# Expert loop of a fused two-block kernel: odd experts' input weights in four places of their own, TensorE looping over pairs of experts

## The reference, cut to what matters

```python
logits = hf @ w_router + b_router            # 32 experts, 4 chosen for a token
gates = softmax(top_k(logits, 4))
for each expert e, over the tokens that chose it:
    hc = xi @ w1[e] + b1[e]                  # 1024 -> 2048: gate and up
    g, u = hc[:, :1024], hc[:, 1024:]
    g = minimum(g, 7); u = clip(u, -7, 7)
    hm = (u + 1) * (g * sigmoid(1.702 * g))
    y += gate * (hm @ w2[e] + b2[e])         # 1024 -> 1024
x = x + g2 * y;  out = rms_norm(x, final_g)
```

## Time and profile before

| what | value |
|---|---|
| device time, median of 3 runs | 2288.06 us (2286.08 to 2289.45) |
| profiled execution: span from first to last instruction | 2379.3 us |
| profiled execution less the median of the runs shown | 91.2 us |
| busy, share of that span | PE 87%, DVE 41%, ACT 23%, POOL 21% |
| read from HBM | 782.55 MB, of which the 192 expert units 402.7 MB |
| passes in the expert loop | 33 (one expert of the 32 has two) |
| first matmul of the expert loop, last of it | 1409.9 us and 2372.0 us |

### The profile page before, as it was taken

The page is one execution under the profiler, slowest core; times in us unless marked ns, Lnnn a source line. Parts: engine busy times, 40 slices in busy tenths (PEclk is TensorE's granted clock), DMA queues, the critical chain, the costliest instruction groups (busy, mean ns, idle before and its releaser), DMA issues.

```text
span 2379.3 us, 27257 instructions
## 1 busy us (share of the span) xinstructions
PE 2070.6 (87%) x9038; PEld 1171.1 (49%) x9039; DVE 979.9 (41%) x2276; ACT 555.0 (23%) x1027; POOL 497.6 (21%) x562
## 2 busy tenths in 40 slices
PE   8998998967658576584999989999999999999998
PEld 7867887623223232232678854444444444444443
DVE  5955555646647566473375232111111111111112
ACT  4636301212112111122214222211111111121112
POOL 0000003466666666665300000000000000000000
PEclk9999999988878787896999989999999999999999
DMA  7352586799999999998842428799999999999996
GB/s 301 142 212 80 195 356 262 277 368 344 370 380 344 366 364 353 371 345 327 345 180 107 176 97 372 301 429 429 428 428 428 430 428 428 429 429 428 428 429 280
DMA packets 111703, 784.34 MB, mean 330 GB/s; under 512 B 13056, under 2 KB 13312, under 8 KB 80160
## 3 DMA queue, kind: packets, MB, share of 16 engines
q1 hardware_dynamic: 37920, 515.18, 52.3%
q0 software_dynamic: 73728, 268.47, 29.8%
HBM read 782.55 MB, written 1.05 MB: 329 GB/s over the span
## 4 chain that ended last, share of the span: by engine, by line
PE 75%; issue 11%; DVE 5%; another core or an unknown queue 2%; ACT 2%; POOL 2%; DMA 1%; DVEq 0%; ACTq 0%; POOLq 0%; SPq 0%
PE ps L786 56%; PE ps L945 16%; PE ps L1210 1%; DVE ring L1942 1%; DVE arena L1942 1%; DMA arena<-in_peer_v,arena 1%; PE ps L918 1%; POOL ring L746 1%; POOL ring L744 1%; DMA ring<-in_peer_v,arena 1%; DVE arena L1700 0%; DVE arena L1891 0%; ACT arena L1372 0%; PE ps L1241 0%
## 5 line engine op out<-in xcount | busy, mean ns | idle before, releaser
L786 PE MATMUL ps<-ring,arena 128*64 128x512 f32 (+2 forms) x3336 | 749.5, 589 | 41.8 <-issue 41.7
L786 PEld LDWEIGHTS ps<-ring,arena 128*64 128x64 f32 (+1 forms) x3336 | 262.9, 140 | 501.5 <-issue 500.7
L945 PE MATMUL ps<-ring,arena 128*128 128x512 f32 x768 | 366.5, 635 | 156.8 <-issue 134.7
L786 PE MATMUL ps<-arena,ring 128*128 128x256 f32 (+1 forms) x2272 | 486.2, 373 | 3.8 <-DVE arena L1685 3.2
L786 PEld LDWEIGHTS ps<-arena,ring 128*128 128x128 f32 x2272 | 417.4, 189 | 65.5 <-issue 6.9
L945 PEld LDWEIGHTS ps<-ring,arena 128*128 128x128 f32 x768 | 154.9, 204 | 364.6 <-issue 340.0
L945 PE MATMUL ps<-arena 128*128 128x512 f32 (+2 forms) x600 | 211.3, 599 | 66.5 <-ACT arena L1278 50.6
L1942 DVE CUSTOM_DVE_ANT_0 ring<-ring,ps 128x1024 f32<-128x1024 f32 x192 | 228.1, 1218 | 94.8 <-DMA ring<-in_peer_v,arena 88.5
L1600 ACT COPY arena<-ps 128x512 f32<-128x512 f32 (+1 forms) x165 | 89.2, 541 | 739.6 <-PE ps L786 683.5
L2255 DVE TENSOR_TENSOR arena<-ps,arena 128x512 f32<-128x512 f32 x66 | 45.7, 692 | 438.4 <-PE ps L1210 438.4
L786 PE MATMUL ps<-arena 128*128 128x128 f32 (+4 forms) x1502 | 215.2, 298 | 11.1 <-ACT arena L1262 6.6
(11 more groups left out here) (336 smaller groups left out, 1214.5 us busy)
## 6 DMA issues: line engine op xcount, KB each, us to landing
ring<-in_w_exp SPq DMA_DIRECT2D x192, 2048.0 KB, 17.1
ring<-in_w_in SPq DMA_DIRECT2D x24, 2048.0 KB, 9.5
ring<-in_w_ada SPq DMA_DIRECT2D x12, 2048.0 KB, 8.8
ring<-in_w_out SPq DMA_DIRECT2D x4, 2048.0 KB, 8.2
ring<-in_w_peer_q SPq DMA_DIRECT2D x4, 2048.0 KB, 10.6
ring<-in_w_br_rnn SPq DMA_DIRECT2D x4, 1280.0 KB, 7.4
ring<-in_w_br_attn SPq DMA_DIRECT2D x2, 2048.0 KB, 13.9
ring<-in_peer_u,arena POOLq DMA_INDIRECT x192
```

Of the source, the lines that this page charges most:

```text
L786: return pe.matmul(o, l, r, start=start, stop=stop)
L945: return pe.matmul(o, l, r, start=start, stop=False, skip_group_check=True)
```

## The change

Input weights (units 0 to 3) of odd experts get four more places, numbered 6 to 9: three at the end of the arena's reused part and one over `xT` and `hT`, which are dead by then. Even experts keep ring places 0 to 3. The output weights (units 4 and 5) of all experts still share places 4 and 5. SP now loads the inputs of expert 1 before the loop too, and in its loop, over pairs, those of e + 2 after the `Zg` and `Zu` of e, and the output weights of e + 1 after the `D` of e. PE loops over 16 pairs of experts; within a pair the pass's code stands twice (even and odd), each in an inner loop over that expert's passes, whose bounds PE reads from a new table `passes_to` that DVE writes. The region `M` is carved anew to make room; `final_row` moves to ring place 2 and is loaded after all weights.

```diff
-        arena_words = 27400
+        arena_words = 28608
+        x_start = at["fixed"]
         xT = carve("fixed", KD, T)
         hT = carve("fixed", KD, T)
...
+        more_slots = [arena[:, second + n * SLOT:second + (n + 1) * SLOT] for n in range(3)]
+        more_slots.append(arena[:, x_start:x_start + SLOT])
+        expert_slot = [ring[:, n * SLOT:(n + 1) * SLOT] for n in range(6)] + [more_slots[n] for n in (1, 2, 0, 3)]
+        w1_unit = [[expert_slot[n].rearrange("p (c j) -> p c j", c=KD) for n in places]
+                   for places in ((0, 1, 2, 3), (6, 7, 8, 9))]
+        w2_unit = [expert_slot[n].rearrange("p (c j) -> p c j", j=D) for n in (4, 5)]
+        final_row = expert_slot[2][:, 0:D]
...
-        w_full = [sem(f"expert_unit_loaded_{n}") for n in range(6)]
+        w_full = [sem(f"expert_unit_loaded_{n}") for n in range(10)]
...
-            def load(e, n):
-                sp.dma_start(ring[:, n * SLOT:(n + 1) * SLOT],
-                             a["w_exp"][bass.ds(e, 1), n].rearrange("e p w -> (e p) w")).then_inc(w_full[n], 16)
+            def load(e, n, place):
+                sp.dma_start(expert_slot[place],
+                             a["w_exp"][bass.ds(e, 1), n].rearrange("e p w -> (e p) w")).then_inc(w_full[place], 16)
...
             for n in sorted(range(RING), key=lambda slot: max(m for m in range(n_second) if m % RING == slot)):
+                if n == (n_second - 4) % RING:
+                    B.filled(sp, "o", HB - 1)
+                    load(1, 0, 6)
+                if n == (n_second - 3) % RING:
+                    load(1, 1, 7)
                 if n == (n_second - 2) % RING:
                     sp.wait_ge(s_mrg, 4 + 4)
-                    load(0, 5)
+                    load(0, 5, 5)
                 unit_free(sp, last_in_slot(n, n_second))
-                load(0, n)
+                load(0, n, n)
+            load(1, 2, 8)
+            B.filled(sp, "h3r", 3)
+            load(1, 3, 9)
             sp.wait_ge(s_slots, 1)
+
+            def used(e, job):
+                q = sp.value_load(last_of[0:1, bass.ds(e, 1)].bitcast(I32), min_val=0, max_val=MAX_PASSES - 1)
+                X.filled(sp, q, job)
+
+            with sp.Fori(0, E // 2 - 1) as p:
+                for odd, places in ((0, (0, 1, 2, 3)), (1, (6, 7, 8, 9))):
+                    e = p * 2 + odd
+                    used(e, "Zg")
+                    load(e + 2, 0, places[0])
+                    load(e + 2, 1, places[1])
+                    used(e, "Zu")
+                    load(e + 2, 2, places[2])
+                    load(e + 2, 3, places[3])
+                    used(e, "D")
+                    load(e + 1, 4, 4)
+                    load(e + 1, 5, 5)
+            used(E - 2, "D")
+            load(E - 1, 4, 4)
+            load(E - 1, 5, 5)
             sp.dma_start(final_row, a["final_g"].partition_broadcast(P)).then_inc(s_row, 16)
-            with sp.Fori(1, E) as e:
-
-                q = sp.value_load(last_of[0:1, bass.ds(e - 1, 1)].bitcast(I32), min_val=0, max_val=MAX_PASSES - 1)
-                for job, ns in (("Zg", (0, 1)), ("Zu", (2, 3)), ("D", (4, 5))):
-                    X.filled(sp, q, job)
-                    for n in ns:
-                        load(e, n)
...
-            with pe.Fori(0, total) as q:
-                e = pe.value_load(expert_of[0:1, bass.ds(q, 1)].bitcast(I32), min_val=0, max_val=E - 1)
+            def one_pass(q, pair, odd):
+
                 pe.wait_ge(s_xg, q * 2 + 2)
-                hidden(q, e, 0, "Zg")
-                hidden(q, e, 1, "Zu")
+                hidden(q, pair * 16 + 16, odd, 0, "Zg")
+                hidden(q, pair * 16 + 16, odd, 1, "Zu")
...
-                        pe.wait_ge(w_full[4 + k // 4], e * 16 + 16)
+                        pe.wait_ge(w_full[4 + k // 4], pair * 32 + 16 * odd + 16)
...
+            with pe.Fori(0, E // 2) as pair:
+                for odd in range(2):
+                    begin = pe.value_load(passes_to[0:1, bass.ds(pair * 2 + odd, 1)].bitcast(I32), min_val=0,
+                                          max_val=MAX_PASSES - 1)
+                    end = pe.value_load(passes_to[0:1, bass.ds(pair * 2 + odd + 1, 1)].bitcast(I32), min_val=1,
+                                        max_val=MAX_PASSES)
+                    with pe.Fori(begin, end) as q:
+                        one_pass(q, pair, odd)
...
                     dve.sem_inc(s_table, 1)
+                    own.mark(dve.memset(passes_to[:, 0:1], 0.0))
+                    own.mark(dve.tensor_copy(passes_to[:, 1:E + 1].bitcast(I32), n_pass[:, 1, :]))
                     own(ts(count, n_pass[:, 1, :], -1.0, None, ALU.add))
```

More of the change, by code:

```diff
@@ L368, in build_program @@
         iota_i, iota16 = carve("fixed", TOPK), carve("fixed", TOPK)
+        dump = carve("fixed", 2)
         def col(name, i=0, n=1):
@@ L481, in build_program @@
         xg = carve("M", KD, P)
+        g2_diag = xg
+        z_start = at["M"]
         z_sb = carve("M", 2, 512)
-        g2_halves = carve("M", 512)
[L484 to L488, removed]
+        at["Z"] = z_start
+        slots4_i = carve("Z", 4 * P)
+        before = carve("Z", P)
+        table = carve("Z", 2, E)
+        gT = carve("Z", T)
+        pass_i, pass_no = carve("Z", 2), carve("Z", 2)
+        assert at["Z"] <= at["M"]
+        g2_halves = carve("M", 512)
+        squares_end = at["M"] - 512 + KD * T
         sel = carve("M", TT, P)
         selg = carve("M", TT, P)
[L491 to L501, removed]
+        bias_now = carve("M", 2 * KD)
         logits = carve("M", E + 4)
@@ L507, in build_program @@
         picked = carve("M", TT, E)
-        gT = carve("M", T)
-        smallM = carve("M", 8)
-        total_i = carve("M", 2)
+        slot_of = carve("M", TT, E)
+        n_pass = carve("M", 4, E)
+        hit = carve("M", 2, E)
         of_pass = carve("M", 2, P)
@@ L513, in build_program @@
         last_of = carve("M", E)
-        assert at["M"] <= at["B"]
-        g2_diag = carve("B", KD, P)
-        assert at["B"] <= kept, (at["B"], kept)
+        passes_to = carve("M", E + 2)
+        total_i = carve("M", 2)
+        smallM = carve("M", 8)
+        assert at["M"] <= squares_end
+        at["M"] = squares_end
+        hm = carve("M", 4, P)
+        yg = carve("M", 512)
+        g2_row = arena[:, at["M"]:at["M"] + D]
+        g_act, u_act, sg_act = carve("M", 4, P), carve("M", 4, P), carve("M", 4, P)
+        selgT = carve("M", T)
+        slots4 = carve("M", 4 * P)
+        second = kept - 3 * SLOT
+        assert at["M"] <= second, (at["M"], second)
+        assert at["B"] <= kept, (at["B"], kept)
+        I32 = mybir.dt.int32
+        more_slots = [arena[:, second + n * SLOT:second + (n + 1) * SLOT] for n in range(3)]
[5 more added lines that the diff above has]
+        final_row = expert_slot[2][:, 0:D]
         y_rows = ring[:, 0:TT * D].rearrange("p (a b) -> p a b", b=D)
-        I32 = mybir.dt.int32
-        w1_unit = [ring[:, n * SLOT:(n + 1) * SLOT].rearrange("p (c j) -> p c j", c=KD) for n in range(4)]
-        w2_unit = [ring[:, n * SLOT:(n + 1) * SLOT].rearrange("p (c j) -> p c j", j=D) for n in (4, 5)]
         s_par = sem("params_loaded")
@@ L1192, in filled_by, with hidden @@
                 ins.then_inc(x_full[EXPERT_BANK[job] - 4], 1)
-            def hidden(q, e, n, job):
+            def hidden(q, loaded, odd, n, job):
                 for half in range(2):
-                    pe.wait_ge(w_full[2 * n + half], e * 16 + 16)
+                    pe.wait_ge(w_full[6 * odd + 2 * n + half], loaded)
                 X.claim(pe, q, job)
@@ L1201, in hidden @@
                         last = mm(ps[half * NS:(half + 1) * NS, EXPERT_BANK[job], :], xg[:, c, 0:NS],
-                                  w1_unit[2 * n + half][:, c, :], c == 0, c == KD - 1)
+                                  w1_unit[odd][2 * n + half][:, c, :], c == 0, c == KD - 1)
                 filled_by(last, job)
@@ L1566, in _ @@
                     if i == 0:
-                        fn(smallB[:, 23:24], eps[:, 1:2], ACT.Sqrt)
+                        fn(dump[:, 0:1], eps[:, 1:2], ACT.Sqrt)
                     act.wait_ge(s_x1, 4 + i + 1)
```

## The result

The changed kernel takes 2275.09 us in the median of 4 runs (2270.96 to 2278.43); the kernel before 2288.76 us. The ratio is 0.9946, with a 95% interval from 0.9930 to 0.9961. Run again, it took 2274.19 us, a ratio of 0.9939 (0.9926 to 0.9951).

A forecast was written before the change was run, and what follows sets the result against it. PE was taken to bound the first passes and the weight stream the rest of the expert loop. A 9.4 us gain less 1.0 us of entry made -8.4 us, 2279.7 us (-0.37%); range 2278 to 2290 us.

The forecast's parts named there:

- The bound and the shape: Expert loop: PE paces early passes, weights the rest; afterwards D is late from about expert 9, the 22 us pause stays.
- first five passes: Expert loop of the kernel before: PE sets the pace for these passes at 27.64 us each, the weights for all others.
- The entry: PE entering the expert loop: three register reads and two loop starts cost 1.0 us, bounds 0 and 2.06.
- The turn of PE's loop hidden: PE between experts: leaving an inner loop, two reads and entering another cost 0, covered by the sequencer's lead.
- the loads ahead hidden: Before the loop: expert 1's four units, 19.6 us of DMA, cost 0; rival that they delay something, 2284.6 us, chance 0.04.
- DVE's two operations and the final row free: Before the loop, some 0.2 us each under DVE's 3.70 us wait; at the end, a load wanted at 2372: both hidden.
- the term 9.4 us: Loop's end: gain of four units' lead, 19.58 us, less 10.15 us because PE has more left after the last late unit.
- the period stays 29.36 us: Steady part of the expert loop: DMA engines never run dry, so each expert still takes 29.36 us after the change.
- The range's lower end, -10: Whole kernel: a free loop entry and no loss would give -10 us, 2278 us.
- The exposed turn: Rival, PE's turn between experts: reads and inner loop not hidden, up to 2317 us; chance 0.13 together with code loading.
- the code fetched again: Rival's twin, PE's jump back over the doubled code: one exposed load of 2.9 us a pair eats the gain; joint chance 0.13.
- an unprofiled stream that is faster than the profiled one: Rival, expert loop: timed loads under 27.75 us an expert leave PE the bound, 2289 us; chance 0.12, partly exposed turns included.

The follow-up runs named there:

- no_head_start: Changed kernel with expert 1's inputs loaded only after the first Zg and Zu, at the head of the loop's stream: 2288.93 us, ratio 1.0001.
- late_up_six: Changed kernel with the up-half loads issued after the output weights in the last three pairs of SP's loop (six experts): 2261.86 us, ratio 0.9894.
- pairs_only: Kernel before with only PE's new pair and inner loops, all weights in the six old places: 2290.53 us, ratio 1.0006.
- dump_first: Changed kernel with dump carved ahead of xT, so the ninth place starts at a multiple of 64 bytes: single run, 2271.68 us.
- shift_only: Kernel before with only the two words dump carved at the end of the arena's fixed part, regions behind moved 8 bytes: ratio 0.9991.
- ring_56_bytes: Kernel before with the ring starting 56 bytes further on, moving all six places: single run, 2288.51 us.

## Why the prediction was right or wrong

**The bound and the shape: right.** Weights set the pace before, PE for the first passes and then weights after (the "first five passes" of the kernel before should be seven: its first wait of 1.5 us is the one that ends at 1613.93, in the eighth pass; no term of the sum hangs on that). The late job is `D`, from expert 10 on (9 or so was said); the stream of loads keeps its pause; the last `D` starts a full pass after the last late unit, so about half of the 19.6 us of lead is lost. The model of the stream also gave the two runs that moved loads around it, `no_head_start` in its first wait and its pause and, once PE's own pace was put back in, `late_up_six` to 1 us.

**The entry: right.** +0.9 us of idle (2.96 and 2.92 against 2.06); 1.0 was said.

**The turn of PE's loop hidden, the loads ahead hidden, DVE's two operations and the final row free: right.** `pairs_only` shows the first; from the block of 456 to the first `Zg` the changed kernel takes 243.1 to 243.9 us and the old one 242.9, so little more than the entry's 0.9 us is new there; from the last `combine` to the end it is 9.3 to 9.4 us in both kernels.

**What failed is the size of the gain in the loop**: the term 9.4 us measured 11.7 (937.5 and 938.0 against 926.3 and 925.8, so 11.3 to 12.2 by pairs of profiles). The mechanism was right, and the step that failed was "the period stays 29.36 us". From 1649.21 to 2205.70 there are 19 experts in 556.49 us, **29.289 us** each; before it was 29.364. The gaps alternate, 29.37 and 29.20 us, and the shorter ones hold the input loads of odd experts, into the arena. Between the pause and the last late unit lie 28 groups of six units, of which 14 hold odd experts' inputs: 14 x 0.165 = 2.3 us, the whole difference. The alternation is in all seven profiles with the arena's places, also in `dump_first` and `no_head_start`; in the kernel before, where the same weights of odd experts go into the ring, the period is 29.36 to 29.37 us throughout, so it isn't where they are read from. The offset of 56 bytes and the ring's address are excluded by the runs; why loads into the arena's places go 0.04 us a unit faster stays open.

**What was left out is the length of the first pass, with its clock.** The granted clock falls to half in the router's stage, where PE is mostly idle. What it does at the loop's entry differs between profiles (columns as in the earlier trace rows; the kernel before, then the changed kernel's first profile, then its second):

```profile
1389.91:1393.91 4.00, 0.66 (x4) 0.42 (x4) 2.74 (x17) 1.50 (x3) 0.00 (x0) 0.88 0.00 0
1393.91:1397.91 4.00, 2.94 (x13) 2.52 (x14) 0.45 (x2) 1.17 (x2) 0.00 (x0) 0.50 0.00 0
...
1409.91:1413.91 4.00, 4.00 (x12) 1.33 (x14) 0.48 (x2) 0.00 (x0) 0.00 (x0) 0.57 0.02 6
```
```profile
1317.10:1321.10 4.00, 4.00 (x10) 1.24 (x12) 0.35 (x2) 0.00 (x0) 0.00 (x0) 0.50 0.02 4
1321.10:1325.10 4.00, 4.00 (x16) 1.19 (x14) 0.00 (x0) 0.00 (x0) 0.00 (x0) 0.76 0.00 0
```
```profile
1317.16:1321.16 4.00, 4.00 (x20) 1.47 (x22) 0.37 (x2) 0.00 (x0) 0.00 (x0) 1.00 0.01 4
```

The first pass takes 22.5, 23.76 and 20.84 us to its `D` in these three. The stretches account for that: 4 x 0.43 = 1.7 us lost in the first, 4 x (0.50 + 0.24) = 3.0 us in the second, nothing in the third. Of the six profiles of the changed kernel and its variants with the head start four have the fast pass and two the longest. Of the six with the old loads two have the fast one (`shift_only`, `ring_56_bytes`) and four a pass of 22.2 to 22.5 us. So the fast pass occurs with the change and without it, and is worth 1.7 us down, the longest 1.2 us up; what decides between them, and whether the change has a part in it, isn't shown.

The sum for the changed kernel's second profile: -11.9 in the loop, -1.7 in the first pass, +0.2 up to its first `Zg` (0.86 of entry less 0.6 before it), so -13.4, near the timed 0.9939. For the first profile it is -11.5, +1.2 and +0.9, so -9.4; that this lies near the forecast's -8.4 is chance: two errors partly cancel. Both first passes may occur among timed runs; how often each does for either kernel the timed runs don't say. The range's lower end, -10, allowed for neither term: it rested on durations of one execution, with one rate for the stream and one length for the first pass.

**The rivals.** The exposed turn and the code fetched again didn't happen. Nothing speaks for an unprofiled stream that is faster than the profiled one: the other profiled executions took 2 us more than their spans and lie among the timed ones, and the 91.2 us were one late execution. The stream's rate rose to 12.583 MB / 29.289 us = 429.6 GB/s in the mean. The Trainium skill's ceiling of 435 GB/s ("DMA: Bandwidth & Descriptors", opening table) agrees: even the shorter periods, of 29.20 us, make 430.9 GB/s. No instruction packet moved after the first three passes. Of the two readings of the Trainium skill, "Runtime: NRT & Kernel Launch", section Instruction fetch mechanics, this bears out the 128 KiB memory of TensorE.

## What to carry to other kernels

When a stream of loads sets the pace, a deeper buffer is worth the lead it gives less what the compute engine must still do after the last unit that is late. Work out which unit that is, and order the last loads so that the compute engine has a stock of work behind it: reordering the loads of six turns, with no new memory, took 9.3 us more off the loop (916.7 against 926.0 us) on top of the 11.7 that came with the four places, and 10 to 13 us off the timed runs. One late unit moved alone gives only the difference of the two paces, 1.7 us here. And a wait of the engine can cost more than its length: the one of 6.89 us cost another 2.06 at half clock.

## What the runs showed of the hardware

A read of a register value and the entry of one more loop cost PE's queue 0.9 us at a loop's entry and nothing between blocks of matmuls of 7 us. One stream into SBUF ran at 428.4 GB/s in periods whose six loads all go to the ring (29.37 us) and at 430.9 in those with four of them to the arena (29.20 us); neither an offset of 56 bytes nor the ring's address showed a cause. Three profiles of two kernels had three lengths of the same first pass, 20.84, 22.5 and 23.76 us, with granted clocks from 0.50 to 1.00 in its first 4 us. One profiled execution, the first of the kernel before, was 96 us (4%) longer than its second, nearly all of it in the stretch of POOL's gathers in the first block; the loop repeated within 0.5 us.
